# Two layers of a hybrid diffusion backbone on one core: the residual stream between the layers

## The chip, the core and the metric

The kernel runs on one core of one Trainium2 chip. Time is device time in microseconds (us). Three runs of the kernel before took 932.32, 935.01 and 936.65 us; their median, 935.01 us, is the number that the change is measured against. Everything is in float32.

## The reference

There are 256 context tokens and 256 latent tokens of width 1024, and two layers. Each layer is a mixer (layer 0: convolution and pooling; layer 1: two kinds of attention) and then a mixture of experts, both with a normalisation that is scaled and shifted by conditioning vectors ahead, and a gated residual behind. The part that matters here is the end of layer 0 and the start of layer 1, where the experts' output is added to the residual stream and the sum is normalised, scaled and shifted again:

```python
y2 = moe(jnp.concatenate([h2c, h2l], axis=1), router_w, router_b,
         moe_w_gate[i], moe_w_up[i], moe_w_down[i])
xc = xc + mod_c[5] * y2[:, :n_ctx]
xl = xl + mod_l[:, 5] * y2[:, n_ctx:]
# next layer
mod_l = (c_act @ mod_w[i] + mod_b[i]).reshape(b, N_MOD, 1, d)
hl = modulate(rms_norm(xl, norm_g[i, 0]), mod_l[:, 0], mod_l[:, 1])
```

The experts stand in 8 groups of 4. A token goes to one group, and in it to two experts. So each of the 512 rows of the residual is added to by exactly one group.

## The kernel before, in words

The weights are the bulk of the traffic. The queue of SP (SyncE) loads them in the order of a list, `STREAM`, 2 MB a unit, into seven slots of a ring and into buffers lent for a time: `X` (which holds the residual in the mixers and an expert's weights in the expert phase), `B`, and pieces of `hT`, `GB`, `MR` and `WORK`. Before each load SP waits for the last user of the slot. SP works strictly in order: whatever one load waits for holds up all that stand behind it.

In the expert phase of layer 0 the residual lies in DRAM. `save_rows` writes it to the tensor `x_old` before `X` is lent out. For each group the rows of its tokens, up to 64 in a first tile and 64 in a second, are gathered, multiplied by the group's gate and up matrices (`gate_up`, L1329) and by its down matrices (`down`, L1354) on PE. A tile lies as 128 partitions: partition 0 to 63 hold the first halves of 64 rows and 64 to 127 the second halves. `out_rows` on DVE then scales the product by the output gate (L2225) and adds the old rows (L2231), which GpSimd has gathered from `x_old` (`take_old`, L897). GpSimd scatters the new rows into a second DRAM tensor, `x_new` (`put_new`, L904). Both are indirect DMAs on GpSimd's queue. A group whose second tile is empty skips it by a branch on every engine (`late_second`). A scatter and a gather are issued for the second tile all the same; their rows are out of bounds and move nothing.

When all eight groups are stored and the branch for overfull groups is passed (`overflow_pool`, not taken with these inputs), GpSimd raises `moe_done`. SP waits for that with the loads of `X` from `x_new` (L1037), which stand in its order ahead of `("oin", "ckv")`, the first projection weights of layer 1. The two loads `("mod", 1, 1, 0)` and `("mod", 1, 1, 1)`, the scale vector's weights of layer 1, stand ahead of that wait and are issued while the experts still run.

Then layer 1 begins. ACT squares the four tiles of `X` (L1564) and copies the product of the scale weights (`mod_copy(7)`, L1570) between the second and the third tile; GpSimd forms the inverse root of the mean square (L2346, L2347); DVE scales the tiles (L1972) and forms the norm's scale (L1931, L1965). PE multiplies the scale weights (`mod(7)`, L1075, 16 trace rows for each 2 MB half), turns their product into columns (L1085), turns the scaled tiles into 16 blocks (L1125), and ACT and DVE copy the blocks out by turns with scale and shift (`hcols`, L1591 and L1995). The first projection of layer 1 (L497) needs all 16 blocks of the first stretch. PE's order there is `mod(7)` first, then the blocks.

## Time and profile before

| | |
|---|---|
| median of the three runs | 935.01 us |
| profiled execution | 934.93 us |
| its span (first to last instruction) | 933.2 us |
| PE busy | 833.0 us (89%) |
| DVE, ACT, POOL busy | 371.4, 164.6, 170.7 us |
| DMA over the span | 317 GB/s mean, 296.08 MB |
| granted TensorE clock, mean | 0.954 |

The profile comes from one execution. Times in its rows count from the start of the span; the execution is 1.7 us longer than the span. PEclk is the granted TensorE clock as a share of full speed: 1.00 is 2.4 GHz and 0.50 is 1.2 GHz. PE appears in two rows, the multiplications (PE) and the weight loads that overlap them (PEld); a name with a q behind it (SPq, POOLq) is the engine's sequencer or the DMAs that it issues. In the bracket at the end of a timeline row stand the idle time of that engine before the row and what ended it.

### The profile page before, as it was taken

What the parts mean: (1) busy time and instruction counts of PE and PEld (TensorE: products, weight loads), DVE (VectorE), ACT (ScalarE), POOL (GpSimd) and SP (SyncE); (2) the same over time, 40 slices, a digit from 0 to 9 for tenths busy, and PEclk for the clock granted to TensorE, in tenths of its full rate; (3) what the DMA queues carried; (4) which work ended last, traced back from release to release, by engine and by line L of the source; (5) the groups of instructions that cost most, each with busy time, mean ns of one, the idle gap of its engine ahead of it and who ended that gap; (6) DMA issues with size and microseconds to landing.
All of it is one profiled execution on the core that took longest, in us unless ns stands there. A gap on an engine that the chain in (4) does not pass through costs nothing.

```text
span 933.2 us, 9923 instructions
## 1 busy us (share of the span) xinstructions
PE 833.0 (89%) x3695; PEld 369.4 (40%) x3695; DVE 371.4 (40%) x785; ACT 164.6 (18%) x409; POOL 170.7 (18%) x205
## 2 busy tenths in 40 slices
PE   4899999999999999887949999979897999979785
PEld 2444445447433333222318544536545333322221
DVE  1279998216121212110114488457645122212110
ACT  2301012216100000000013111436612000000000
POOL 2100292131120222201122231320220100000000
PEclk9999999999999999898967999989996999999999
DMA  8999355627999999999979467521294899999994
GB/s 362 409 418 403 135 210 218 270 90 245 330 399 424 352 399 399 400 396 416 424 299 428 185 260 292 249 91 40 114 388 159 341 425 425 420 426 428 426 422 175
DMA packets 31463, 296.08 MB, mean 317 GB/s; under 512 B 6050, under 2 KB 6356, under 8 KB 13229
## 3 DMA queue, kind: packets, MB, share of 16 engines
q1 hardware_dynamic: 25200, 283.26, 75.0%
q0 software_dynamic: 6128, 12.02, 3.6%
q8 instruction: 38, 0.62, 0.3%
q14 instruction: 21, 0.16, 0.0%
q10 hardware_dynamic: 76, 0.02, 0.0%
HBM read 291.84 MB, written 11.53 MB: 325 GB/s over the span
## 4 chain that ended last, share of the span: by engine, by line
PE 52%; DMA 18%; DVE 13%; issue 6%; SPq 4%; ACT 2%; PEld 2%; POOL 1%; another core or an unknown queue 0%; PEldq 0%; DVEq 0%; POOLq 0%; ACTq 0%
PE bank L1329 15%; DVE WORK L2301 10%; PE bank L497 9%; PE bank L1354 6%; PE bank L1479 5%; DMA WORK<-in_gu_pack 5%; DMA ring<-in_gu_pack 4%; DMA ring<-in_down_pack 4%; DMA ring<-in_win_pack 3%; PE bank L1191 3%; SPq L1016 2%; PE bank L1426 2%; PE bank L1267 2%; DMA WORK<-x_old,smalli 1%; PE bank L554 1%
## 5 line engine op out<-in xcount | busy, mean ns | idle before, releaser
L1329 PE MATMUL bank<-ring,WORK 128*64 128x512 f32 x352 | 107.3, 627 | 12.0 <-DMA ring<-in_gu_pack 7.5
L1329 PE MATMUL bank<-ring,hT 128*64 128x512 f32 x352 | 108.0, 616 | 3.7 <-issue 2.2
L2301 DVE SCALAR_TENSOR_TENSOR WORK<-WORK,par 128x512 f32<-128x512 f32 x116 | 90.7, 861 | 0.0
L497 PE MATMUL bank<-ring,hT 128*128 128x512 f32 (+2 forms) x256 | 88.0, 499 | 0.7 <-ACT hT L1591 0.7
L1354 PE MATMUL bank<-ring,WORK 128*64 128x512 f32 x336 | 76.3, 596 | 2.3 <-DMA ring<-in_down_pack 1.2
L2210 DVE SCALAR_TENSOR_TENSOR hT<-hT,WORK,bank 128x256 f32<-128x256 f32 x18 | 8.7, 481 | 167.4 <-ACT hT L1628 161.1
L2210 DVE SCALAR_TENSOR_TENSOR WORK<-WORK,bank 128x256 f32<-128x256 f32 x16 | 7.7, 481 | 137.3 <-ACT WORK L1628 137.3
L1633 ACT ACTIVATE WORK<-bank 128x256 f32<-128x256 f32 x34 | 13.1, 384 | 268.3 <-PE bank L1338 268.3
L497 PEld LDWEIGHTS bank<-ring,hT 128*128 128x128 f32 x256 | 46.0, 190 | 35.9 <-issue 34.0
L1426 PE MATMUL bank<-hT,ring 128*128 128x512 f32 x128 | 57.7, 610 | 2.0 <-DMA ring<-in_win_pack 2.0
L1479 PE MATMUL bank<-ring,B 128*128 128x512 f32 x128 | 56.6, 596 | 0.8 <-DVE B L2318 0.8
L1329 PEld LDWEIGHTS bank<-ring,WORK 128*64 128x64 f32 x352 | 31.7, 143 | 61.6 <-issue 61.3
L1329 PEld LDWEIGHTS bank<-ring,hT 128*64 128x64 f32 x352 | 31.8, 141 | 45.0 <-issue 44.8
L2346 POOL TENSOR_SCALAR small<-small 128x1 f32<-128x1 f32 (+2 forms) x46 | 13.5, 294 | 182.7 <-DVE small L1792 62.6
L1075 PE MATMUL bank<-ring,cs 128*32 128x512 f32 x256 | 34.1, 670 | 9.5 <-DMA ring<-in_mod_pack 8.3
L1329 PE MATMUL bank<-WORK,hT 128*64 128x512 f32 x72 | 36.1, 649 | 7.3 <-issue 5.7
L904 POOL DMA_INDIRECT latents<-WORK,smalli x8 | 8.1, 1014 | 181.8 <-DVE WORK L2231 153.1
L1354 PEld LDWEIGHTS bank<-ring,WORK 128*64 128x64 f32 x336 | 23.2, 137 | 45.2 <-issue 40.6
L1426 PEld LDWEIGHTS bank<-hT,ring 128*128 128x128 f32 x128 | 24.6, 194 | 33.6 <-issue 31.3
L891 POOL DMA_INDIRECT hT<-h_rows,smalli x14 | 13.4, 960 | 129.7 <-PE bank L1303 56.0
L2347 POOL TENSOR_TENSOR small<-small,cst 128x1 f32<-128x1 f32 (+2 forms) x46 | 36.1, 785 | 3.8
L1479 PEld LDWEIGHTS bank<-ring,B 128*128 128x128 f32 x128 | 23.8, 190 | 31.2 <-issue 27.7
(337 smaller groups left out, 1215.5 us busy)
## 6 DMA issues: line engine op xcount, KB each, us to landing
ring<-in_gu_pack SPq DMA_DIRECT2D x39, 2048.0 KB, 20.5
ring<-in_mod_pack SPq DMA_DIRECT2D x24, 2048.0 KB, 12.2
ring<-in_down_pack SPq DMA_DIRECT2D x19, 2048.0 KB, 24.9
WORK<-in_gu_pack SPq DMA_DIRECT2D x5, 2048.0 KB, 22.9
ring<-in_wout_pack SPq DMA_DIRECT2D x4, 2048.0 KB, 12.1
ring<-in_gu_pack SPq DMA_DIRECT2D x8, 1024.0 KB, 34.8
ring<-in_win_pack SPq DMA_DIRECT2D x3, 2048.0 KB
X<-in_gu_pack SPq DMA_DIRECT2D x3, 2048.0 KB
```

What stands on the lines that cost most here:

```text
L497: mm = pe.matmul(dst[:, 0:hi - lo], hT[:, k, t * P:(t + 1) * P], w[:, k, :], start=k == 0, stop=k == KC - 1)
L1016: sp.dma_start(dst, src).then_inc(sem(f"weights_in{at}"), 16)
L1075: mm = pe.matmul(bank[b][at:at + 32, :], cs[:, k, :], w, start=k < 2, stop=k >= KC - 2)
L1191: mm = pe.matmul(bank[OUT_BANKS[L][i % 2]][:, :], lhs(k, j), w[:, k, :], start=k == 0, stop=k == KC - 1)
L1267: mm = pe.matmul(bank[7 - 7 * h][:, w * k:w * k + w], X[:, 2 + t, at:at + P] if L else B[:, t * D + at:t * D + at + P], FIRST[:, w * t:w * ...
L1329: mm = pe.matmul(dst[ST * x:ST * x + ST, :], HG[L][s][:, k, :], columns(units[x], 512 * k, 512), start=k == 0, stop=k == KC - 1)
L1354: mm = pe.matmul(bank[5 + s][ST * h:ST * h + ST, :], HET[s][:, f, ST * x:ST * x + ST], columns(n, 2048 * x + 1024 * f + 512 * h, 512), sta ...
L1426: mm = pe.matmul(b[:, :], w[:, k, 256 * part + P * (m % 2):256 * part + P * (m % 2) + P], hT[:, k, :], start=k == 0, stop=k == KC - 1)
L1479: mm = pe.matmul(bank[OUT_BANKS[0][i % 3]][:, :], mixT[:, (k + 4) % KC, j * P:(j + 1) * P], w[:, (k + 4) % KC, :], start=k == 0, stop=k == ...
L2210: dve.scalar_tensor_tensor(out=T1[L][s], in0=SG[L][s], scalar=cwt[:, at:at + 1], in1=src[:, 0:DE], op0=ALU.mult, op1=ALU.mult).then_inc(se ...
L2301: ins = dve.scalar_tensor_tensor(out=acc, in0=src, scalar=w, in1=acc, op0=ALU.mult, op1=ALU.add)
L2347: pool.tensor_tensor(dst, dst, C("half", 0, 1).to_broadcast([P, n]), ALU.pow).then_inc(sem(name), 1)
```

## The change

Three things are done. First, the rows of groups 0 to 6 are scattered back into the tensor that they were gathered from (now `x_rows`), and `x_new` is gone; GpSimd stores seven groups, not eight, and raises `moe_done` after the seventh. Second, SP's wait for `moe_done` and the reload of `X` stand ahead of `("mod", 1, 1, 0)`, with a wait for the last expert unit that lay in `X`. Third, the rows of group 7 never go to DRAM: DVE builds one-hot matrices from the token numbers of the group's tiles (`last_places`, eight comparisons of 128x128, after group 6's rows), PE multiplies them with the gated rows (`spread_last`: eight products of 64 rows by 128 tokens by 512 columns, 16 where the second tile is in use), and DVE adds the eight results, 128x512 each, to the reloaded `X`.

What follows from it in the orders: PE turns the first four blocks of the scaled tiles ahead of `mod(7)`; ACT squares all four tiles ahead of `mod_copy(7)`; DVE scales all four tiles ahead of the norm's scale. Group 7's gather of old rows, its addition (L2231) and its scatters are gone. The overflow branch gets a buffer of its own and a few waits; it is not taken.

The diff, cut to its core:

```diff
-        xa = nc.dram_tensor("x_old", (TOK, D), F32, kind="Internal").ap()
-        xb = nc.dram_tensor("x_new", (TOK, D), F32, kind="Internal").ap()
+        xa = nc.dram_tensor("x_rows", (TOK, D), F32, kind="Internal").ap()
...
+        LAST_HOT = [hw[:, 1024 + 512 * i:1536 + 512 * i] for i in (0, 1)]
+        last_tok = csg[:, 0:2]
+        SPREAD = [(t, h) for t in range(NT) for h in (0, 1)]
+        SPREAD_BANKS = (0, 1, 2, 3, 4, 5, 7, 6)
...
# SP
-                if u == ('oin', 'ckv'):
-
+                if u == ("mod", 1, 1, 0):
+                    done, v = freed(max(i for i in range(n) if PLACES[i][0] == X_SLOT))
+                    expert_slot_freed(sp, 0, done, v)
                     sp.wait_ge(sem("moe_done"), 1)
                     for t in range(NT):
-                        sp.dma_start(X[:, t, :], xb[t * P:(t + 1) * P, :]).then_inc(sem(("x_in", "x_back")[t // 2]), 16)
+                        sp.dma_start(X[:, t, :], xa[t * P:(t + 1) * P, :]).then_inc(sem(("x_in", "x_back")[t // 2]), 16)
                 load(n, load_sources(u) if u[0] not in ("gu", "down") else expert_sources(u[1], u[2], n, u[0]))
...
# PE
+            def spread_last():
+
+                def products(tiles):
+
+                    for n, (t, h) in enumerate(SPREAD):
+                        half = slice(ST * h, ST * h + ST)
+                        for i in range(tiles):
+                            mm = pe.matmul(bank[SPREAD_BANKS[n]][:, :], LAST_HOT[i][half, t * P:t * P + P], YO[i][half, :], start=i == 0, stop=i == tiles - 1)
+                        mm.then_inc(sem("ln_turned"), 1)
 
                 for i in range(2):
-                    turn_pair(tag, i, range(KC))
+                    pe.wait_ge(sem(f"y_used_{i}"), GROUPS)
+                last = second_tile(pe, 0, GROUPS - 1)
+                with pe.If(last > 0):
+                    products(2)
+                with pe.Else():
+                    products(1)
+                pe.nop()
...
             overflow_pe(pe, 0)
-
+            spread_last()
+
+            turn_pair("a1", 0, range(4))
             mod(7)
-            turn_x("a1")
+            turn_pair("a1", 0, range(4, KC))
+            turn_pair("a1", 1, range(KC))
...
# ACT
-            square_rows("a1", (0, 1))
+            square_rows("a1", range(4))
             mod_copy(7)
-            square_rows("a1", (2, 3))
...
# DVE
+                    if L == 0 and g == GROUPS - 1:
+                        return
                     if L == 0:
                         dve.wait_ge(sem(f"old_in_{s}"), 16 * g + 16)
...
+                def last_places():
+
+                    for i in range(2):
+                        for t in range(NT):
+                            ins = ts(LAST_HOT[i][:, t * P:t * P + P], C("iota128"), last_tok[:, i:i + 1], float(NOROW - t * P), ALU.subtract, ALU.is_equal)
+                    link(ins)
...
             overflow_vector(dve, 0)
+            for n, (t, h) in enumerate(SPREAD):
+                dve.wait_ge(sem("ln_turned"), 2 * NT + n + 1)
+                dve.wait_ge(sem(("x_in", "x_back")[t // 2]), (96, 32)[t // 2])
+                x = X[:, t, 512 * h:512 * h + 512]
+                tt(x, x, bank[SPREAD_BANKS[n]][:, :], ALU.add).then_inc(sem("x_added"), 1)
             norm_rows("a1")
...
# GpSimd
-                for g in range(GROUPS):
+                for g in range(GROUPS - 1 + L):
                     if L == 0 and g + 2 < GROUPS:
                         gather(g + 2)
                     store(g)
-                    if L == 0 and g + 1 < GROUPS:
+                    if L == 0 and g + 2 < GROUPS:
                         old_rows(g + 1)
```

SP's order at the end of layer 0 and the start of layer 1, before. The two units `in_mod_pack` are the scale weights of layer 1, `in_oin_pack` are its projections:

```order
L1012 DMA ring<-in_down_pack 128x2048 [waits gu_done_1,gu_done_0]
L1013 DMA ring<-in_down_pack 128x2048
L1016 DMA ring<-in_mod_pack 128x4096 [waits down_done_1,down_done_0]
L1016 DMA ring<-in_mod_pack 128x4096 [waits gu_done_1,gu_done_0]
L1037 DMA X<-x_new 128x1024 [waits moe_done]
L1037 DMA X<-x_new 128x1024 x3
L1016 DMA ring<-in_oin_pack 128x1536 [waits down_done_1,down_done_0]
```

And of the changed kernel:

```order
L1021 DMA ring<-in_down_pack 128x2048 [waits gu_done_1,gu_done_0]
L1022 DMA ring<-in_down_pack 128x2048
L1047 DMA X<-x_rows 128x1024 [waits moe_done,gu_done_1,gu_done_0]
L1047 DMA X<-x_rows 128x1024 x3
L1025 DMA ring<-in_mod_pack 128x4096 [waits down_done_1,down_done_0]
L1025 DMA ring<-in_mod_pack 128x4096 [waits gu_done_1,gu_done_0]
L1025 DMA ring<-in_oin_pack 128x1536 [waits down_done_1,down_done_0]
```

The reload and its wait have gone past the two scale weight units, which now stand behind both.

PE's order between the experts' last branch and the first blocks, before (`weights_in4` and `weights_in3` are the two halves of the scale weights, `xs` counts scaled tiles):

```order
L842 UNCONDITIONAL_BRANCH
L1075 MATMUL bank<-ring,cs 32x512 [waits weights_in4,mod_rows]
L1075 MATMUL bank<-ring,cs 32x512 x7
L1075 MATMUL bank<-ring,cs 32x512 [waits weights_in3]
L1075 MATMUL bank<-ring,cs 32x512 x7
L1085 MATMUL bank<-cst,MR 128x4 [waits mod_cols,mod_rows]
L1085 MATMUL bank<-cst,MR 128x4 x3
L1125 MATMUL bank<-cst,B 128x128 [waits xs]
L1125 MATMUL bank<-cst,B 128x128 x7
L1125 MATMUL bank<-cst,B 128x128 [waits ht_0]
```

And of the changed kernel:

```order
L765 TENSOR_LOAD smalli [waits y_used_1,y_used_0]
L765 ISA x2
L1151 COMPARE_AND_BRANCH
L1145 MATMUL bank<-WORK,hT 128x512 x16
L1151 UNCONDITIONAL_BRANCH
L1145 MATMUL bank<-WORK,hT 128x512 x8
L1153 UNCONDITIONAL_BRANCH
L1135 MATMUL bank<-cst,B 128x128 [waits xs]
L1135 MATMUL bank<-cst,B 128x128 x7
L1085 MATMUL bank<-ring,cs 32x512 [waits weights_in4,mod_rows]
L1085 MATMUL bank<-ring,cs 32x512 x7
L1085 MATMUL bank<-ring,cs 32x512 [waits weights_in3]
```

Ahead of the scale weights' product now stand a branch, the eight or sixteen spreading products and the first eight transposes, with their waits for group 7's rows and for two scaled tiles.

## Rows read from the trace of the kernel before

**Rows 1.** Chain that ended last, 452 to 500: start, us, what.
```profile
456.46 1.00 POOL x_new L904
457.77 11.33 DMA WORK<-x_old,smalli
...
472.41 5.28 DMA x_new<-WORK,smalli
...
478.67 6.59 DMA X<-x_new
...
485.29 2.19 ACT B L1564 x4
...
498.29 0.57 ACT hT L1591
...
499.37 0.73 PE bank L497 x3
```

**Rows 2.** Timeline of PE, 440 to 512: start, us, engine, line, op, count.
```profile
464.54 3.65 PE L1354 MATMUL bank<-ring,WORK 128*64 128x512 f32 x16 [0.56 <-ACT WORK L1633]
471.15 2.89 PE L1075 MATMUL bank<-ring,cs 128*32 128x512 f32 x16 [2.96 <-DMA ring<-in_mod_pack]
477.08 3.64 PE L1075 MATMUL bank<-ring,cs 128*32 128x512 f32 x16 [3.05 <-DMA ring<-in_mod_pack]
...
493.73 4.96 PE L1125 MATMUL bank<-cst,B 128*128 128x128 f32 x22 [1.61 <-DVE hT L1995]
```

**Rows 3.** Timelines of ACT and of DVE in the same stretch.
```profile
487.38 0.57 ACT L1570 ACTIVATE MR<-bank 128x512 f32<-128x512 f32 x1
...
490.51 0.56 ACT L1591 ACTIVATE hT<-bank,mods,gsc 128x256 f32<-128x256 f32 x1 [0.47 <-PE bank L1125]
...
494.88 0.56 ACT L1591 ACTIVATE hT<-bank,mods,gsc 128x256 f32<-128x256 f32 x1 [2.16 <-PE bank L1125]
...
462.25 0.75 DVE L2222 SCALAR_TENSOR_TENSOR WORK<-GB,WORK 128x512 f32<-128x512 f32 x1 [0.68 <-DMA x_new<-WORK,smalli]
468.31 0.69 DVE L2225 TENSOR_TENSOR WORK<-bank,WORK 128x512 f32<-128x512 f32 x1 [5.31 <-PE bank L1354]
...
491.81 1.41 DVE L1972 TENSOR_SCALAR B<-X,small 128x1024 f32<-128x1024 f32 x1 [0.72 <-POOL small L2347]
```

**Rows 4.** The scatter that GpSimd issues at 456.46: KB, us to landing.
```profile
x_new<-WORK,smalli POOLq DMA_INDIRECT x1, 9.1
```

**Rows 5.** SP's timeline of DMA issues, 340 to 520.
```profile
439.84 2.47 SPq L1016 DMA_DIRECT2D ring<-in_mod_pack  x2
...
480.41 3.56 SPq L1016 DMA_DIRECT2D ring<-in_oin_pack  x5
```

**Rows 6.** The reload of X: issue ns, first and last start, landing.
```profile
L1037 SPq DMA_DIRECT2D X<-x_new x4: 327/432/693, 478.3 to 479.9; - x4
...
DMA to landing us min/median/max: 3.2/6.5/7.9
```

**Rows 7.** Stretches: length, busy by engine, then PEclk, DMA share, GB/s.
```profile
464.00:470.00 6.00, 3.65 (x16) 1.23 (x16) 1.11 (x2) 0.38 (x1) 0.00 (x0) 1.00 1.03 426
472.00:475.00 3.00, 2.03 (x12) 0.27 (x4) 0.00 (x0) 0.00 (x0) 1.11 (x2) 0.50 0.75 301
475.00:479.00 4.00, 1.92 (x12) 0.59 (x16) 0.00 (x0) 0.00 (x0) 0.00 (x0) 0.50 0.08 28
479.00:484.00 5.00, 1.73 (x12) 0.00 (x0) 0.00 (x0) 0.00 (x0) 0.00 (x0) 0.50 0.92 251
484.00:490.00 6.00, 1.99 (x10) 1.99 (x11) 1.59 (x3) 4.71 (x9) 2.78 (x6) 0.50 1.03 425
```

**Rows 8.** Timeline of PE around 160: the same multiplication earlier, both halves.
```profile
160.28 3.64 PE L1075 MATMUL bank<-ring,cs 128*32 128x512 f32 x32
```

**Rows 9.** PE's groups of instructions at 617 to 660: busy, mean ns.
```profile
L563 PE MATMUL bank<-B,WORK 64*128 64x512 f32 x32 | 9.0, 641 | 0.0
```

**Rows 10.** Timeline of PE at 423 to 424: a wait behind a branch.
```profile
423.94 1.09 PE L1329 MATMUL bank<-WORK,hT 128*64 128x512 f32 x1 [5.71 <-issue]
```

More of the change, by code:

```diff
@@ L375, in generator_kernel @@
         rcol = wk[:, 2092:2114]
-        ROWS_IN = (("old_in_0", 16 * GROUPS), ("old_in_1", 16 * GROUPS), ("gathered_0", 16 * (GROUPS - 1)))
+        ROWS_IN = tuple((name, 16 * (GROUPS - 1)) for name in ("old_in_0", "old_in_1", "gathered_0"))
         FIRST = YO[0]
@@ L841, in overflow_pe @@
                         mm.then_inc(sem(f"over_down{L}"), 1)
+                    if L == 0:
+                        pe.wait_ge(sem("over_rows0"), j + 2)
             with pe.Else():
@@ L876, in overflow_vector @@
                     if L == 0:
-                        gate = YO[0]
+                        gate = OYO
                         dve.scalar_tensor_tensor(out=gate, in0=GM[1], scalar=msk[:, bass.ds(j + 8 * c, 1)], in1=GM[0],
@@ L880, in overflow_vector @@
                         dve.wait_ge(sem(f"over_t1{L}"), steps * j + 3)
-                    dve.tensor_tensor(YO[0], bank[5][:, :], gate, ALU.mult).then_inc(sem(f"over_t1{L}"), 1)
+                    y = (OYO, YO[0])[L]
+                    dve.tensor_tensor(y, bank[5][:, :], gate, ALU.mult).then_inc(sem(f"over_t1{L}"), 1)
                     dve.wait_ge(sem(f"over_t1{L}"), steps * j + steps)
-                    dve.tensor_tensor(YO[0], YO[0], XR[L][0], ALU.add).then_inc(sem(f"over_rows{L}"), 1)
+                    dve.tensor_tensor(y, y, XR[L][0], ALU.add).then_inc(sem(f"over_rows{L}"), 1)
             with dve.Else():
@@ L898, in take_old, with put_new @@
                                            bounds_check=2 * rows_ - 1, oob_is_err=False)
-        def put_new(pool, L, s, i):
+        def put_new(pool, L, src, i):
             rows_ = moe_plan(L)[0] * P
-            dst = (xb, out[0])[L].rearrange(HALVES, h=2)
-            return pool.indirect_dma_start(dst, bass.IndirectOffsetOnAxis(ap=smalli[:, i:i + 1], axis=0), YO[s], None,
+            dst = (xa, out[0])[L].rearrange(HALVES, h=2)
+            return pool.indirect_dma_start(dst, bass.IndirectOffsetOnAxis(ap=smalli[:, i:i + 1], axis=0), src, None,
                                            bounds_check=2 * rows_ - 1, oob_is_err=False)
@@ L909, in overflow_pool @@
             with pool.If(n > 0):
+                if L == 0:
+                    pool.wait_ge(sem("hg_turned_0"), turned_by(0, GROUPS - 1))
                 with pool.Fori(0, n) as j:
@@ L1018, in save_rows @@
             def save_rows(L):
-                sp.wait_ge(sem("x_added"), (8, 12)[L])
+                sp.wait_ge(sem("x_added"), (8, 20)[L])
                 for j, t in enumerate(x_tiles(f"m{L}")):
@@ L1977, in norm_rows @@
                 if tag == "a1":
-                    for j in (0, 1):
+                    for j in range(4):
                         scaled(tag, j)
@@ L1981, in norm_rows @@
                     norm_scale(1, 0)
-                    for j in (2, 3):
-                        scaled(tag, j)
                 for i in range(2):
@@ L2033, in add_out @@
                         if i >= 2:
-                            dve.wait_ge(sem("x_added"), 8 * L + i - 1 + last)
+                            dve.wait_ge(sem("x_added"), 16 * L + i - 1 + last)
                         if L == 1 and i < 2:
@@ L2166, in route @@
                 if L == 0:
+                    dve.tensor_copy(last_tok, bank[6][:, GROUPS * c - c:GROUPS * c])
                     ts(smalli[:, 4:4 + ntile], bank[6][:, 0:ntile], float(NOROW), None, ALU.add)
@@ L2218, in out_rows @@
                     if G0 + g:
-                        dve.wait_ge(sem(f"y_stored_{s}"), 16 * (G0 + g))
+                        dve.wait_ge(sem(f"y_stored_{s}"), 16 * ((GROUPS - 1) * L + g))
                     if L == 0:
@@ L2251, in experts @@
                             late_second(g - 1)
+                        if L == 0 and g == GROUPS - 1:
+                            last_places()
                     if L == 1 and q == 0 and g + 1 < GROUPS:
@@ L2384, in store @@
                     for s in range(c):
-                        pool.wait_ge(sem(f"y_rows_{s}"), 8 * L + g + 1)
-                        put_new(pool, L, s, 48 + g * c + s).then_inc(sem(f"y_stored_{s}"), 16)
+                        pool.wait_ge(sem(f"y_rows_{s}"), (GROUPS - 1) * L + g + 1)
+                        put_new(pool, L, YO[s], 48 + g * c + s).then_inc(sem(f"y_stored_{s}"), 16)
                 def old_rows(g):
@@ L2390, in old_rows @@
                         if g:
-                            pool.wait_ge(sem(f"y_rows_{s}"), 8 * L + g)
-                            pool.wait_ge(sem(f"old_in_{s}"), 128 * L + 16 * g)
+                            pool.wait_ge(sem(f"y_rows_{s}"), g)
+                            pool.wait_ge(sem(f"old_in_{s}"), 16 * g)
                         take_old(pool, L, s, 48 + g * c + s).then_inc(sem(f"old_in_{s}"), 16)
@@ L2405, in take_group @@
                     if g > 2:
[L2406 removed]
+                        pool.wait_ge(sem("y_rows_0"), GROUPS - 1 + g - 2)
                     take_old(pool, 1, g % 3, 48 + g).then_inc(sem(ROWS_IN[g % 3][0]), 16)
@@ L2426, in experts @@
                 for s in range(c):
-                    pool.wait_ge(sem(f"y_stored_{s}"), 128 * (L + 1))
+                    pool.wait_ge(sem(f"y_stored_{s}"), 16 * (GROUPS - 1 + GROUPS * L))
                 overflow_pool(pool, L, n)
```

13 lines of the change are left out of this document (6 added, 7 removed).

## The prediction, made before the changed kernel was run

> **What bounds the kernel now.** I read first the chain that ended last, because the change touches one seam of the program and only the chain says what the seam costs. Between the last experts and layer 1 it runs through single transfers, not through a busy engine [rows 1]: a scatter of group 6 at 456.46, a gather of old rows behind it that takes 11.33 us, the scatter of group 7 at 472.41 that takes 5.28, the reload of X (6.59), two squares on ACT, and then the blocks up to the first projection at 499.37. The DVE timeline shows that the gather is no price of its own: group 7's product is ready for DVE only at 468.31, when PE has ended its last down product [rows 2, 3], and the gather came 1.1 us later. What the seam really costs is everything between 468.2 and 499.37, some 31 us in which PE does little.
>
> The second view is the PE timeline, since the change also moves the scale weights of layer 1. PE waited for each of their 2 MB halves, until 471.15 and until 477.08, though SP had issued both by 442.3 [rows 2, 5]. The third view, the stretches, says why [rows 7]: the DMA engines move 426 GB/s in 464 to 470 and run dry only around 475. So the queue is full of expert weights until shortly before, and the scale weights are what fills it from then to 475. Then it stands empty until the reload starts (28 GB/s in 475 to 479). The scale product ended at 480.7 but its copy stood on ACT behind two squares until 487.38 [rows 3]. In the old kernel the scale weights thus have 6.7 us of slack, and the rows are late.
>
> **The change part by part.** Every time below is in the profiled execution, 934.93 us (span 933.2 and 1.7 around it); the median of the runs shown is 935.01, so the two can be exchanged within 0.1.
>
> *Part 1, moe_done earlier.* The stores of group 6 now end the expert phase. The second starts at 456.46 and lands 9.1 us later, at 465.6 [rows 4]; the first has landed by 462.25, where DVE's wait for it ended [rows 3]. Group 7's scatter, in an almost idle queue, took 5.28 [rows 1]. So the second store lands between 462.3 (just behind the first) and 465.6. The queue stays loaded until about 463.8 (475 minus the 4.19 MB of scale weights and 0.4 MB of the rest at the rates of rows 7), so I take 464.8, near the loaded row. From landing to SP's first issue it was 0.6 us (472.41 + 5.28 = 477.7 to 478.3 [rows 1, 6]). The reload starts at 465.4, bounds 462.9 and 466.2, instead of 478.3: 12.9 us earlier.
>
> *Part 2, the scale weights behind the reload.* They are issued 26 us later than before, and the queue order puts X's 2.10 MB ahead of them. From its first issue at 478.3 the old reload had moved at most 5 x 251 GB/s = 1.26 MB by 484, and the other 0.84 MB at 425 GB/s takes 2.0 us: 7.7 us in all [rows 7]. The 4.19 MB of scale weights follow at 425: 9.9 us. From the last byte to PE's start was 2.1 us before (about 475 to 477.08). So the second half is there at 465.4 + 7.7 + 9.9 + 2.1 = 485.1, the first 4.9 earlier, at 480.2. Before, it was 477.08: the scale weights lose 8.0 us, more than their slack. Bounds: DMA without a gap from 463.8 and all 6.29 MB at 425 gives 463.8 + 14.8 + 2.1 = 480.7; reload at 466.2 and X at 251 GB/s throughout (0.7 to start, 8.4 to move) gives 487.3.
>
> Beside that row stands a rule of the Trainium skill, "DMA: Bandwidth & Descriptors", section on the anatomy of one DMA: a transfer costs about 2.0 us plus its bytes at 436 GB/s, whatever it is. By it the reload and the weights together would take an estimated 16.4 us and arrive at 481.8, so that the time would be 3.3 us lower than my sum. The row of 251 GB/s while X's rows are read speaks against it, the 2.1 us at the end speaks for it.
>
> *Part 3, from the scale weights to the projection.* The product of the second half took 3.64 us at the half clock (0.50 in 475 to 479, 1.2 GHz); earlier in the kernel both halves together took 3.64 [rows 2, 8], so 1.82 at full clock. PE will again have waited just before it, as in the nearer row: I take 3.64. Copy to the first block on ACT: 487.38 to 490.51, 3.13, and 0.1 for PE to ACT. The blocks go at 494.88 to 498.29 in four steps, 0.85 each; eight blocks per engine take 7 x 0.85 + 0.56, and 0.5 more until PE starts, 7.0 in all. Before it was 8.9 (490.51 to 499.37), because DVE scaled the last tile at 491.81 and PE waited 1.61 for its block [rows 2, 3]; all four tiles are now scaled early, which gives 1.9 back. The projection starts at 485.1 + 3.64 + 0.1 + 3.13 + 7.0 = 499.0, against 499.37.
>
> *Part 4, group 7's rows on chip.* YO is gated at 469.0 (468.31 + 0.69). The branches on DVE and on PE I cost like GpSimd's from landing to SP, 0.6 each: first product at 470.2. Eight products are 16 trace rows of 64 x 512; 32 such rows were 9.0 us busy [rows 9], so 4.5 us, or 9.0 at the half clock. The granted clock fell while PE idled at the same place, so I take the middle, to about 477. The last tile of X lands by 9.5 us after the first issue (7.9 behind the last issue [rows 6]), at 474.9, so it waits for nothing. The last addition, 0.7 like any 128x512, ends at 477.7; two scaled tiles at 0.75 make 479.2; eight transposes at 4.96 / 22 make 481.0. The first half of the scale product, which stands behind them on PE, is done at 484.6 at worst. That is 0.5 us ahead of the second half's arrival: hidden, but barely. If all products run at the half clock it is 1.7 us too late, at full clock 2.8 early.
>
> *Free edits.* The eight comparisons on DVE lie between group 6's rows and 460.6, where DVE otherwise idles behind PE; without that cover they would be about 2 us. Group 7's gather and scatters are off the queue, each at most 64 rows of 4 KB, 0.6 us at 425 GB/s. The loads of the projections, before issued at 480.41 [rows 5], come right behind the scale weights, about 2 us earlier than before, and PE did not wait for them. Everything behind the first projection moves with it, since the loads there are triggered by PE's own progress.
>
> Sum: 499.0 - 499.37 = -0.4 us, 934.5. Bounds of this case: 480.7 and full clock, 492.6 (-6.7); 487.3 and half clock, 501.2 (+1.8).
>
> **The rivals.** *Early data.* The store lands right behind the first one, X flows at the full 425 GB/s since its queue never runs dry, and PE keeps its clock through the products. Then the second half is there at 480.7 and the projection starts at 492.7: -6.7, 928.3. For it speaks that the queue was idle only because nothing was issued; against it the measured 251 GB/s under the reload, and the clock that fell to 0.50 at this place with the same idle time ahead [rows 7].
>
> *A stall at the new branch (slower).* At 423.94 PE stood 5.71 us behind a branch with nothing that the profile names as its reason [rows 10]; the queue was full then, as it will be at 470 with X in flight. If PE's sequencer stands like that at the branch in the spreading, the transposes and the first half of the scale product move 5.7 us back, to 490.3, and the second half follows at 3.64: projection at 504.2, +4.8. With all products at the half clock 2.3 more: +7.1, 942.0. It decides from 0.5 us of delay on, and most other branches on PE passed without such a stall.
>
> *The change moves work, not the end.* That is my forecast itself: the scale weights take the place of the rows.
>
> **How the numbers follow.** My forecast has a chance of 0.68, the early data 0.18, the stall 0.14. What a measurement can tell from no change is about 0.5%, 4.7 us; the forecast lies inside it but for its lowest bound, which is the first rival; the two rivals lie outside. So faster 0.18, same 0.68, slower 0.14. The range reaches half way into either rival: 929.0 to 940.0. The likeliest case's own range is 931.5 (second half 3 us sooner, or the scale product at full clock and 1 us sooner) to 937.
>
> **What would show it.** SP's reload would start near 465.4 and the two scale units right behind it. PE's second half of L1075 (its line in the new kernel is L1085) would start near 485, ended by a DMA, and the copy on ACT would follow it at once, not behind squares. The products would stand at 470 to 477, the four additions of late tiles would wait for PE and not for X, and the wait of PE for DVE between the blocks would be gone. Wrong would be: a reload that starts before 463, a second half before 482, or an idle stretch of PE over 3 us between the last down product and the first spreading product. And should a wait in layer 1 absorb or add to a shift at the first projection, the end of the run would not follow it; the rows show none.

## The result, and the profile after

The changed kernel took 927.99 us (median of 6 runs, 926.33 to 931.1), the kernel before 934.20 beside it (6 runs). The ratio is 0.9936, with a 95% interval of 0.9921 to 0.9950: 6.0 us faster, and no less than 4.7. A second measurement of it on another chip (after_again, below) gave 0.9949, 0.9931 to 0.9967: some 4.8 us. The prediction, 934.5 and most likely no change, was wrong; its range ended at 929.0. One run of e3_one_product, below, took 2340.01 us and is left out of that kernel's ratio, not of its median. The profiled execution of the changed kernel took 929.5 us (span 927.7, mean granted clock 0.962), 5.4 less than the profiled one of before.

The chain of waits of the changed kernel, 454 to 500, shows what stands in place of the chain of before [rows 1]. Columns: start, us, what.

```profile
456.92 6.85 DMA x_rows<-WORK,smalli
...
464.42 0.33 SPq L1047
...
466.95 17.19 DMA ring<-in_mod_pack
...
484.18 1.97 PE bank L1085 x16
...
486.17 0.60 ACT MR L1597
...
486.82 1.07 PE bank L1095 x8
...
488.40 0.57 ACT hT L1618
...
494.47 5.60 PE bank L501 x33
```

The gather, the second scatter, the reload and the squares have left the chain. Group 6's store, SP's reload, the second half of the scale weights, its product, and the blocks stand there instead, as Parts 1 to 3 of the prediction have it. But the first projection starts at 494.47, not at 499.0; before it was 499.37 [rows 1]. Behind it nothing is given back: the span is shorter by 5.5 us, the start of the first projection by 4.9.

The store at the head of this chain carries nothing: it is that of group 6's second tile, which is empty (both stores of the group moved 0.22 MB, and a full tile is 0.26). DVE's wait for the first store ended at 462.52, 1.2 us before the second landed:

```profile
462.52 0.75 DVE L2247 SCALAR_TENSOR_TENSOR WORK<-GB,WORK 128x512 f32<-128x512 f32 x1 [0.54 <-DMA x_rows<-WORK,smalli]
```

What waiting for the empty store costs isn't shown; no run leaves it out.

PE in the same stretch, with the idle time ahead of a row and what ended it in the bracket. L1378 is the last down product, L1145 the spreading products, L1135 the blocks (L1125 before), L1085 the two halves of the scale product (L1075 before), L1095 its turning (L1085 before), L501 the first projection (L497 before):

```profile
464.95 3.68 PE L1378 MATMUL bank<-ring,WORK 128*64 128x512 f32 x16 [0.56 <-ACT WORK L1660]
470.86 5.40 PE L1145 MATMUL bank<-WORK,hT 64*128 64x512 f32 x16 [2.24 <-issue]
479.04 1.97 PE L1135 MATMUL bank<-cst,B 128*128 128x128 f32 x8 [2.78 <-DVE B L1998]
480.94 2.60 PE L1085 MATMUL bank<-ring,cs 128*32 128x512 f32 x16
484.18 1.92 PE L1085 MATMUL bank<-ring,cs 128*32 128x512 f32 x16 [0.64 <-DMA ring<-in_mod_pack]
486.82 1.05 PE L1095 MATMUL bank<-cst,MR 128*128 128x4 f32 x8 [0.72 <-ACT MR L1597]
489.11 4.68 PE L1135 MATMUL bank<-cst,B 128*128 128x128 f32 x24 [1.24 <-ACT hT L1618]
494.47 7.71 PE L501 MATMUL bank<-ring,hT 128*128 128x192 f32 x46 [0.69 <-ACT hT L1618]
```

The second half of the scale product takes 1.92 us where it took 3.64 [rows 2]. The stretches of the changed kernel (columns as in [rows 7]; the two numbers behind the engines' are the granted clock and the DMA share) show at which clock:

```profile
472.00:475.00 3.00, 3.00 (x10) 1.11 (x10) 2.57 (x4) 1.36 (x3) 0.33 (x2) 0.52 1.04 437
...
477.00:479.00 2.00, 0.00 (x0) 0.00 (x0) 1.98 (x4) 1.79 (x4) 1.19 (x2) 0.99 0.96 410
479.00:481.00 2.00, 1.96 (x12) 1.63 (x16) 0.86 (x2) 0.00 (x0) 1.69 (x3) 0.50 1.09 467
...
483.00:485.00 2.00, 1.36 (x16) 0.29 (x12) 0.00 (x0) 0.00 (x0) 0.00 (x0) 1.00 1.02 428
485.00:487.00 2.00, 1.28 (x14) 0.31 (x6) 0.00 (x0) 0.60 (x1) 0.00 (x0) 1.00 1.03 436
...
489.00:492.00 3.00, 2.89 (x14) 2.92 (x15) 1.52 (x4) 2.02 (x4) 0.66 (x1) 0.53 1.03 437
```

Before, the clock stood at 0.50 in every stretch from 472 to 490, and the DMA engines stood nearly still in 475 to 479 [rows 7]. Now the DMA engines move over 400 GB/s there, and the clock is 1.00 from 483 to 487: just when the second half and its turning run. Ahead of that PE had blocks and the first half to do without a gap from 479.04 to 483.5; which of its work brings the clock back is asked of the experiments.

SP's issues and the four late additions on DVE answer to [rows 5, 6] and to Part 4:

```profile
464.42 1.90 SPq L1047 DMA_DIRECT2D X<-x_rows  x4
466.41 0.91 SPq L1025 DMA_DIRECT2D ring<-in_mod_pack  x2
467.42 3.06 SPq L1025 DMA_DIRECT2D ring<-in_oin_pack  x5
```

```profile
472.02 1.28 DVE L2368 TENSOR_TENSOR X<-X,bank 128x512 f32<-128x512 f32 x2 [2.58 <-PE bank L1145]
...
475.18 2.48 DVE L2368 TENSOR_TENSOR X<-X,bank 128x512 f32<-128x512 f32 x4 [0.42 <-PE bank L1145]
```

SP issues the reload at 464.42 and the two scale units right behind it. The additions wait for PE, not for X, and end at 477.66, where 477.7 was forecast.

### The profile page after: what moved, and what is told of

Its sections match the earlier page's. It is cut to its first block, busy times and chain, and to the rows that moved or that the text cites. A ratio compares the mean times of both kernels' runs of the same rounds, so it can differ in the third digit from the quotient of the medians.

```text
span 927.7 us, 9974 instructions
## 1 busy us (share of the span) xinstructions
PE 835.6 (90%) x3711; PEld 369.9 (40%) x3711; DVE 376.5 (41%) x801; ACT 164.6 (18%) x409; POOL 166.6 (18%) x201
## 4 chain that ended last, share of the span: by engine, by line
PE 54%; DMA 20%; DVE 13%; issue 5%; SPq 3%; ACT 2%; PEld 2%; POOL 0%; another core or an unknown queue 0%; PEldq 0%; DVEq 0%; POOLq 0%; ACTq 0%
PE bank L1353 15%; DVE WORK L2337 10%; DMA ring<-in_gu_pack 9%; PE bank L501 9%; PE bank L1378 6%; PE bank L1503 5%; DMA WORK<-in_gu_pack 5%; DMA ring<-in_win_pack 3%; PE bank L1215 3%; SPq L1025 2%; DMA ring<-in_mod_pack 2%; PE bank L1450 2%; PE bank L1291 2%; PE bank L558 1%; PE bank L567 1%
## 5 line engine op out<-in xcount | busy, mean ns | idle before, releaser
L501 PE MATMUL bank<-ring,hT 128*128 128x512 f32 (+2 forms) x256 | 88.0, 500 | 0.7 <-ACT hT L1618 0.7
L1378 PE MATMUL bank<-ring,WORK 128*64 128x512 f32 x336 | 76.3, 596 | 1.0 <-ACT WORK L1660 1.0
L501 PEld LDWEIGHTS bank<-ring,hT 128*128 128x128 f32 x256 | 46.0, 190 | 35.7 <-issue 33.9
L1378 PEld LDWEIGHTS bank<-ring,WORK 128*64 128x64 f32 x336 | 23.1, 137 | 43.9 <-issue 40.6
L1450 PEld LDWEIGHTS bank<-hT,ring 128*128 128x128 f32 x128 | 24.6, 195 | 33.6 <-issue 31.2
L1085 PE MATMUL bank<-ring,cs 128*32 128x512 f32 x256 | 32.1, 637 | 4.0 <-DMA ring<-in_mod_pack 2.8
```

The lines of the kernel that those rows point to most:

```text
L501: mm = pe.matmul(dst[:, 0:hi - lo], hT[:, k, t * P:(t + 1) * P], w[:, k, :], start=k == 0, stop=k == KC - 1)
L1085: mm = pe.matmul(bank[b][at:at + 32, :], cs[:, k, :], w, start=k < 2, stop=k >= KC - 2)
L1378: mm = pe.matmul(bank[5 + s][ST * h:ST * h + ST, :], HET[s][:, f, ST * x:ST * x + ST], columns(n, 2048 * x + 1024 * f + 512 * h, 512), sta ...
L1450: mm = pe.matmul(b[:, :], w[:, k, 256 * part + P * (m % 2):256 * part + P * (m % 2) + P], hT[:, k, :], start=k == 0, stop=k == KC - 1)
```

## The experiments

I asked two things: is the gain due to the order on the queue (theory A), and where do the 4.5 us between 499.0 and 494.47 come from? For the clock I had three answers: the blocks and the first half, an unbroken run on PE, bring it back (B); the spreading products do (C, the rival); and whichever it is, without both the second half runs at the half clock as forecast (D; against it E, that the second half runs at the full clock whatever PE did before). Each kernel is timed against the kernel before on the same chip. In the table "gap" is the time from the end of the last down product to the first projection, in the one profiled execution of each.

| kernel | median, us | ratio to before, 95% | gap, us |
|---|---|---|---|
| before | 934.2 to 934.9 | 1 | 31.2 |
| e1_weights_first | 935.84 | 1.0013, 0.9998 to 1.0027 | 31.9 |
| e5_before_busy | 933.69 | 1.0001, 0.9980 to 1.0022 | 29.5 |
| e6_done_late | 933.88 | 0.9997, 0.9982 to 1.0013 | 29.0 |
| e4_products_twice | 932.72 | 0.9981, 0.9968 to 0.9994 | 26.5 |
| e7_half_ahead | 930.77 | 0.9949, 0.9932 to 0.9967 | 26.5 |
| e10_one_product_blocks_behind | 930.59 | 0.9951, 0.9933 to 0.9969 | 26.2 |
| changed kernel, first time | 927.99 | 0.9936, 0.9921 to 0.9950 | 25.8 |
| e11_banks_turned | 929.62 | 0.9953, 0.9935 to 0.9970 | 25.4 |
| e3_one_product | 929.27 | 0.9950, 0.9933 to 0.9967 | 24.7 |
| e2_blocks_behind | 928.74 | 0.9941, 0.9920 to 0.9961 | 24.1 |
| after_again (the changed kernel) | 929.81 | 0.9949, 0.9931 to 0.9967 | 23.3 |
| e8_half_ahead_blocks_behind | 927.29 | 0.9913, 0.9895 to 0.9931 | 22.8 |
| e8_again | 926.66 | 0.9917, 0.9899 to 0.9935 | 22.8 |

The gap orders the kernels nearly as their times do, so this stretch, the seam between the layers, is where they differ. It does so within some 3 us: the changed kernel itself has 25.8 and 23.3 in two executions.

**The order on the queue (e1_weights_first).** Everything changed, but the reload stands behind the scale weights again:

```diff
-                if u == ("mod", 1, 1, 0):
+                if u == ("oin", "ckv"):
```

> The changed kernel with SP's order of before: both halves of the scale weights are issued while the experts run, the reload of X behind moe_done. All else as changed. Theory A (the arrival of the scale weights, 19.7 us behind the first issue of the reload, ends the seam): the weights now arrive at about 471 and 477, X about 10 us later than in the changed kernel, last tile near 482; additions end near 483, two scaled tiles near 484.5, and PE's order (four blocks, then the scale product, 3.8 us at full clock) puts the first projection at 498 to 499, 3.5 to 4.5 us later than in the changed kernel, about 932. Rival (where the reload stands in SP's order is nothing, the rows stay on chip and that is the gain): first projection within 1 us of 494.5, about 928.

The whole gain is gone, more than theory A had forecast (about 932). In its timelines of DVE and of PE, group 7's additions now wait for X, and PE for the tiles:

```profile
479.14 5.02 DVE L2368 TENSOR_TENSOR X<-X,bank 128x512 f32<-128x512 f32 x8 [9.64 <-DMA X<-x_rows]
```

```profile
485.54 1.97 PE L1135 MATMUL bank<-cst,B 128*128 128x128 f32 x8 [10.92 <-DVE B L1998]
487.44 4.63 PE L1085 MATMUL bank<-ring,cs 128*32 128x512 f32 x32
```

The reload was issued at 466.72, as early as in the changed kernel within 2.3 us; it came late because 4.2 MB of scale weights lay ahead of it. Storing in place and spreading on chip are worth nothing without the order. The reverse, the order without the rows of group 7 on chip, wasn't run.

**The time of the release (e6_done_late).** `moe_done` is raised only once group 7's product is ready, 4.9 us later:

```diff
+                if L == 0:
+                    pool.wait_ge(sem("y_used_0"), GROUPS)
                 pool.sem_inc(sem("moe_done"), 1)
```

> The changed kernel, but GpSimd raises moe_done only when DVE has gated group 7's rows, so that the reload starts near 470 and not at 464.4: 5.5 us later, with nothing else changed. Theory A: everything behind follows one for one: second half of the scale weights 19.7 us behind the first issue, first projection 5 to 6 us later, near 500, time 933 to 934, the whole gain gone. Rival (PE's rows path through the products is the bound and the reload has slack): 0 to 2 us later.

The reload's first issue is at 469.31 (464.42 in the changed kernel), and PE's second half still waits for its weights:

```profile
487.20 1.92 PE L1085 MATMUL bank<-ring,cs 128*32 128x512 f32 x16 [0.90 <-DMA ring<-in_mod_pack]
...
497.31 4.95 PE L501 MATMUL bank<-ring,hT 128*128 128x192 f32 x29 [0.70 <-ACT hT L1618]
```

So the date of group 6's store goes through to the end, though not one for one: of the 4.9 us at the reload 3.0 are left at the second half, which came 17.9 us behind the first issue and not 19.8, and 2.8 at the projection. In the times the whole gain of some 6 us is gone. Profile and times differ mostly by which executions were profiled: the two, 932.76 and 929.5, are 3.3 us apart, but e6's lies 1.1 us under its kernel's median and the changed kernel's 1.5 over its own.

**How much the rows can be late (e4_products_twice).** PE does the spreading products twice:

```diff
-                    for n, (t, h) in enumerate(SPREAD):
+                    for again in (0, 1):
+                        for n, (t, h) in enumerate(SPREAD):
...
```

> The changed kernel with all eight spreading products computed twice into the same banks; the additions wait for the second. It measures what slack the rows have behind the scale weights (the forecast: 0.5 us). Theory A with that slack: the products end 4 us later, near 480, the additions near 481.5, the blocks and the first half move by 3.5 to 4 us, the second half starts at 487 to 488 behind PE's own work, first projection 2.5 to 3.5 us later, time about 931. Rival (the scale weights alone end the seam, the rows have several us of slack): within 1 us of the changed kernel.

```profile
471.90 7.14 PE L1146 MATMUL bank<-WORK,hT 64*128 64x512 f32 x32 [2.22 <-issue]
...
483.77 5.34 PE L1085 MATMUL bank<-ring,cs 128*32 128x512 f32 x32
```

The two halves of the scale product now run without a wait for DMA: the rows are late, as was expected. The projection starts 3.6 us later than in after_again on the same chip, the median is 2.9 higher, for products that end 3.8 later. So the slack there is some 0.2 us, and the forecast of 0.5 was the right size.

**What brings the clock back (e2, e3, e10).** e2 puts the blocks behind the scale product, so that PE has no transposes ahead of it. e3 makes one spreading product only, whose bank all eight additions read, so that seven products are left out of the result; e10 does both.

```diff
# e2, e10
-            turn_pair("a1", 0, range(4))
+            pe.wait_ge(sem("x_added"), 16)
             mod(7)
-            turn_pair("a1", 0, range(4, KC))
+            turn_pair("a1", 0, range(KC))
# e3, e10
-                    for n, (t, h) in enumerate(SPREAD):
+                    for n, (t, h) in enumerate(SPREAD[:1]):
...
```

> The changed kernel with PE's order of before at one place: the whole scale product ahead of the blocks (PE waits for all eight additions first, because the product's banks are those of the last two), and no block turned early. Theory B (the run of transposes and the first half of the product just ahead of the second half brings the granted clock back to 1.00, and that is worth 2.6 us of product and turning): without the transposes the first half runs alone and PE waits longer before the second; granted clock 0.50 in the second half, which takes 3.6 us and the turning 1.9, first projection 2.5 to 4 us later than 494.5. Rival (the clock follows the spreading products, which are still there): second half at 1.9 us, only the four blocks in front are lost, 0.5 to 1 us later.

> The changed kernel with one of the eight spreading products; all eight additions read its bank, so the other seven products are left out of the result. PE is then idle from about 471.5 until the first blocks near 478. Theory B: the clock of the second half comes from the run of blocks and first half, not from the products, so it is full there as before (1.9 to 2.4 us) and the first projection stays within 1 us of 494.5. Rival C (the products keep the clock up for the scale product): granted clock 0.50 through the second half, 3.6 us, turning 1.9, first projection 2.5 to 3.5 us later although the additions end earlier.

> Both of the last two edits at once in the changed kernel: one spreading product whose bank all eight additions read (seven products left out of the result), and the whole scale product ahead of the blocks. PE then idles from about 471.5 to 478 and again between the two halves, as the forecast had assumed. Theory D (either run of PE work, the products or the blocks with the first half, keeps the granted clock at 1.00 for the second half, and the forecast's mis-sized term is that half at 3.64 us with the turning at 1.87): now the clock is 0.50, second half 3.6, turning 1.9, first projection 2.5 to 3.5 us later than with the products (492.7), at 495 to 496.5. Rival E (the second half runs at full clock here whatever PE did before): 1.9 us, first projection within 0.7 us of 492.7.

PE of e2, of e3 and of e10, from the scale product to its turning, and behind the dots a stretch in which the second half runs:

```profile
478.30 1.92 PE L1085 MATMUL bank<-ring,cs 128*32 128x512 f32 x16 [2.05 <-DVE X L2368]
482.69 1.92 PE L1085 MATMUL bank<-ring,cs 128*32 128x512 f32 x16 [2.47 <-DMA ring<-in_mod_pack]
485.33 1.06 PE L1095 MATMUL bank<-cst,MR 128*128 128x4 f32 x8 [0.72 <-ACT MR L1597]
...
483.00:485.00 2.00, 1.61 (x16) 0.26 (x8) 0.00 (x0) 0.32 (x1) 0.00 (x0) 1.00 1.03 435
```

```profile
481.76 4.89 PE L1085 MATMUL bank<-ring,cs 128*32 128x512 f32 x32
487.38 1.05 PE L1095 MATMUL bank<-cst,MR 128*128 128x4 f32 x8 [0.73 <-ACT MR L1597]
...
485.00:487.00 2.00, 1.65 (x16) 0.24 (x8) 0.00 (x0) 0.27 (x1) 0.00 (x0) 1.00 1.09 459
```

```profile
479.22 3.64 PE L1085 MATMUL bank<-ring,cs 128*32 128x512 f32 x16 [6.22 <-DMA ring<-in_mod_pack]
484.06 3.40 PE L1085 MATMUL bank<-ring,cs 128*32 128x512 f32 x16 [1.20 <-DMA ring<-in_mod_pack]
488.19 1.06 PE L1095 MATMUL bank<-cst,MR 128*128 128x4 f32 x8 [0.72 <-ACT MR L1597]
...
485.00:487.00 2.00, 2.00 (x16) 0.31 (x8) 0.00 (x0) 0.00 (x0) 0.00 (x0) 0.50 1.14 482
```

e2 shows that B is not needed: with the products alone the clock is 1.00 in its stretches from 475 to 487, and both halves take 1.92. The delay of the projection that both answers expected isn't seen (492.74, against 494.47 and 492.57 of the changed kernel). e3 shows that C is not needed either: its clock is 0.50 from 475 to 483, while PE waits for the rows until 479.86 and then starts on the blocks, and back at 1.00 from 485, after the blocks and the first half; the two halves take 4.89 together, where 7.04 is e10's sum. Take both away and D comes true for the second half: the clock of e10 is 0.50 from 475 to 487, and the second half takes 3.40 us, near the 3.64 of the forecast. So either of two things that the change itself gives PE to do brings the clock back ahead of the second half. D's other half fails: the turning was to take 1.9 us and took 1.06, at a clock of 0.98 in 487 to 489. So the lost clock costs e10 time in the second half alone. e10 is 1.85 us slower than e2, both timed on one chip; the second half's own difference is 3.40 - 1.92 = 1.5. The two intervals overlap, so the size rests on the durations.

**The clock alone (e5_before_busy).** The kernel before, with 20 small products on PE between the scale product and its turning, to bring the clock back without the change:

```diff
-            mod(7)
+            mod_multiply(7)
+            for i in (0, 1):
+                pe.wait_ge(sem(f"y_used_{i}"), GROUPS)
+            busy(5, 20)
+            mod_turn(7)
```

> The kernel before, with 20 small products (128x128 with a constant) on PE between the scale product and its turning, where PE idled for 6.7 us behind the squares; nothing else changed. It measures the granted clock by itself. Theory D: the clock is 1.00 when the turning starts, so it takes 1.05 and not 1.87, and blocks are turned at full clock: first projection 0.8 to 1.5 us earlier than 499.37, time 0 to 1.5 us below the kernel before. So the clock alone is no more than a third of the gain in the old order, since there the rows are late. Rival (the clock is most of the gain): 3 us or more.

Its PE (lines as in the kernel before):

```profile
484.23 1.05 PE L1085 MATMUL bank<-cst,MR 128*128 128x4 f32 x8 [0.22 <-ACT MR L1574]
...
490.83 4.96 PE L1125 MATMUL bank<-cst,B 128*128 128x128 f32 x22 [2.09 <-DVE hT L1999]
```

The turning runs at the full clock, but the blocks still wait for DVE's copies, which stand behind its late tiles, and the clock is 0.50 again from 487 on. The ratio is 1.0001, give or take 0.2%. The gap is 1.7 us shorter in this execution, but its chain doesn't pass through the turning: it goes through the third tile of X, and from that tile's square to the projection it takes 11.1 us, against 11.5 in the kernel before. What the clock shortened here wasn't on the path; it counts only once the scale product bounds the end.

**A finer order (e7, e8, e8_again, after_again, e11).** The first half of the weights needn't be loaded behind the reload. e7 lets it go ahead of the reload; e8 does that and takes the PE order of e2:

```diff
-                if u == ("mod", 1, 1, 0):
+                if u == ("mod", 1, 1, 1):
```

> The changed kernel with the first half of the scale weights issued ahead of the wait for moe_done and only the second half behind the reload. Theory A: the DMA queue no longer stands idle between 463.5 and 466, the second half arrives 2 to 3 us sooner; but PE does four blocks and the first half before it (479 to 483.5), so the first projection gains only 0.6 to 1 us: 493.5 to 494, 927 to 928. Rival (the reload now waits behind the first half and the rows become the bound): X 4 to 5 us later, first projection 1 to 3 us later.

> The last kernel with, in addition, the whole scale product ahead of the blocks on PE. Theory A: the first half is there before the additions end near 478, the second at 479 to 481, so that the product ends near 482, the scale is ready at 485 and the first projection starts at 490.5 to 492, 2.5 to 4 us before the changed kernel's 494.5; time 924.5 to 926.5, below both kernels. Rival (rows are the bound once X waits behind the first half): first projection 493 to 495, no better than the changed kernel.

In e7 the rival comes true, the rows become the bound: the additions wait 4.62 us for X, until 474.90, and PE's first blocks wait for DVE until 481.26. The second half is there early, but stands on PE behind blocks that aren't ready. e8 takes that away, since the scale product runs while DVE and ACT work on the rows. I ran it again beside the changed kernel on another chip:

> The changed kernel itself, on the chip of the next three. Theories A and D: seam and time as in its first profile: second half of the scale weights 18 to 20 us behind the first issue of the reload, both halves at mostly full clock, first projection 494 to 495.5, about 928, ratio 0.993 to 0.995. Rival (the first profile was a lucky execution): 930 or more.

```profile
471.50 3.70 PE L1145 MATMUL bank<-WORK,hT 64*128 64x512 f32 x16 [2.22 <-issue]
...
483.51 1.96 PE L1085 MATMUL bank<-ring,cs 128*32 128x512 f32 x16 [0.16 <-DMA ring<-in_mod_pack]
```

The second half again runs at the full clock; the spreading products, 5.40 us in the first profile, take 3.70. The median, 929.81, lies between theory and rival, and the profiled execution is the fastest of the six.

> The kernel with the first half of the scale weights ahead of the reload and the whole scale product ahead of the blocks, next to the changed kernel. Theory A: 1 to 3 us below the changed kernel. Rival: within 0.5 us of it.

```profile
479.72 5.23 PE L1085 MATMUL bank<-ring,cs 128*32 128x512 f32 x32 [2.94 <-DVE X L2368]
485.68 1.05 PE L1095 MATMUL bank<-cst,MR 128*128 128x4 f32 x8 [0.73 <-ACT MR L1597]
...
491.99 8.04 PE L501 MATMUL bank<-ring,hT 128*128 128x192 f32 x48 [0.69 <-ACT hT L1618]
```

e8 took 926.66 us against 929.81 for the changed kernel on that chip, 3.1 less, and was the fastest on both chips. The intervals of the two ratios overlap a little (0.9899 to 0.9935, and 0.9931 to 0.9967). The products for the scale no longer wait for a transfer but for the additions (2.94 us), because the scale product writes a bank that the additions read until then, and PE waits for all eight of them.

e11 turns the banks so that the wait goes, and lets the scale product start after two of the eight additions (`x_added` already stands at 8 when they begin):

```diff
-        SPREAD_BANKS = (0, 1, 2, 3, 4, 5, 7, 6)
+        SPREAD_BANKS = (6, 7, 0, 1, 2, 3, 4, 5)
...
+            pe.wait_ge(sem("x_added"), 10)
```

> The kernel before in this list with one thing more: the spreading products use banks 6, 7, 0 to 5 in this order, so that the banks of the scale product are those of the first tile's additions, and PE waits for two additions ahead of the scale product and not for eight. Theory A: the first half starts near 477 and not at 480.3, the second ends at 482.5 to 483.5, the scale is ready near 485, and the first projection starts 1.5 to 2.5 us earlier, at 490 to 491; time 1 to 2.5 us below that kernel. Rival (the additions and the squares of the last tile are the bound once X waits behind the first half): no earlier projection, PE waits for the blocks of the second stretch instead.

```profile
475.79 1.92 PE L1085 MATMUL bank<-ring,cs 128*32 128x512 f32 x16
481.15 2.96 PE L1085 MATMUL bank<-ring,cs 128*32 128x512 f32 x16 [3.43 <-DMA ring<-in_mod_pack]
484.80 1.87 PE L1095 MATMUL bank<-cst,MR 128*128 128x4 f32 x8 [0.70 <-ACT MR L1597]
486.53 6.44 PE L1135 MATMUL bank<-cst,B 128*128 128x128 f32 x32
```

```profile
483.00:485.00 2.00, 1.30 (x9) 0.20 (x2) 0.00 (x0) 0.60 (x1) 0.00 (x0) 0.50 1.02 434
```

The first half starts 3.9 us earlier than in e8_again, the turning 0.9, and the projection 1.7 later (493.65). The last down product had ended 0.9 earlier in this execution, so counted from there the turning is no earlier at all and the projection 2.6 later. Neither theory A nor its rival came: the median is 929.62, 3.0 above e8_again on the same chip. With the first half done early PE idles 3.43 us ahead of the second; the clock is 0.50 from 483 to 492, and turning and blocks take 1.87 and 6.44 us where e8_again has 1.05 and some 4.7. What looked like a wait to be removed was what kept the two halves together on PE.

## Why the prediction was wrong, by its own steps

*Part 1, the release: the mechanism right, one term too large.* The store was to land 8.3 us after its issue (464.8 - 456.46), near the loaded row; it took 6.85. The queue ran dry sooner than I had worked out: the DMA engines moved 275 GB/s in 462 to 464 already. Part of that was a slip in the sum: at the rates of the old trace, with 377 GB/s in 470 to 472, the 4.6 MB reach back to 463.1 and not to 463.8. The reload started at 464.42 instead of 465.4, inside the bounds: 1.0 us.

*Part 2, the order on the queue: right.* From the reload's first issue to the second half it was to be 19.7 us; it was 19.76 (484.18 - 464.42). In the other executions with this order and a wait for the weights it was between 17.9 (e6) and 20.1 (e10), so that it agrees to 0.1 us is luck. The rule of the Trainium skill that stood beside this sum ("DMA: Bandwidth & Descriptors", on the anatomy of one DMA, which gives it for DMAs that GpSimd issues, while SP issued these) gives an estimated 16.4 us; no run came so low. e1 shows the price of the other order.

*Part 3, from the weights to the projection: this is the step that failed, in three of its terms.* It took the second half at 3.64 because "PE will again have waited just before it, as in the nearer row". PE did wait just before it, but only 0.64 us, and what counts is what it did before that: blocks and first half without a gap, and before these the spreading products, all of it work that the change had put there. The second half ran at a clock of 1.00 in 1.92 us: 1.7 us less. e10, without that work, has 3.40.

The second term is the way from the copy to the first block, 2.23 us (486.17 to 488.40) and not 3.13, 0.9 less. The 3.13 was read where the turning of the old kernel ran at the half clock, after PE had idled behind ACT's squares (e5, with products in that gap, has 1.05):

```profile
488.01 1.87 PE L1085 MATMUL bank<-cst,MR 128*128 128x4 f32 x8 [7.28 <-ACT MR L1570]
```

The forecast itself had the copy follow the product at once, and left the price as it was; PE idled 0.72 us there, and the turning took 1.05. This term doesn't hang on the clock of the second half: in e10, too, the way takes 2.23 (487.54 to 489.77).

The third: the blocks to the projection took 6.07 and not 7.0, though their clock was 0.53. Four of the sixteen were turned already, so the first two copies on each engine went out within 1.0 us; I had charged each engine eight steps of 0.85. Together with Part 1 this is 1.0 + 1.7 + 0.9 + 0.9 = 4.5, which is 499.0 - 494.5.

The first two of these four stood in the forecast as the lower end of its likeliest case, 931.5 ("the scale product at full clock and 1 us sooner"). Both came true. The other two, priced nowhere, bring this execution down to 929.5, the edge of the range, and the median of its kernel lies 1.5 lower: 6.5 us below the forecast. The second median, 929.81, lies just inside the range. after_again shows an execution in which the blocks too ran at the full clock, with the projection at 492.57.

*Part 4, the rows on chip: right.* Products to 476.26, last addition to 477.66, the first four blocks' turn to 481.0 and the first half to 483.5, against 477, 477.7, 481.0 and 484.6. The slack was 0.64 us, 0.5 by forecast, and e4 shows that it is no more than that order of size. The middle that was taken for the products held by luck, too: they took 5.40 us here, and 3.70 at the full clock in after_again, where 4.5 had been charged for it.

*The rivals.* The early data had a chance of 0.18 and a time of 928.3, which is where the kernel came out, but mostly for other reasons. The full clock in the second half was right (1.92 us). The data ready 4.4 us sooner was not: it was 0.9. The clock kept through the products was not, in this execution: it was 0.52 in 472 to 475, and came back later. I had tied early data and clock together, and outside that rival the clock had only the end of a range.

The stall at the new branch didn't come: the 2.2 us between the last down product and the first spreading product were 2.0 by forecast (468.2 to 470.2), 2.2 to 2.3 in all executions of the changed kernel and its variants. None of the signs that were to show the forecast wrong came, and those that were to show it right did, within 1 us: none of them was the clock of the second half or the price of the turning.

*Left open.* Why the last down product ends between 468.2 and 470.1 in executions of kernels that are the same up to there, and why the spreading products, behind the same wait of 2.2 us, keep the full clock in some executions (3.70 us in after_again, e1 and e7) and lose it for a time in others (5.40 in the first profile, e6, e8 and e11).

## What to carry to other kernels

A duration taken from the old kernel carries that stretch's granted clock with it: before it is put into a sum, ask what the engine will have done just ahead of it in the new order, and give the clock a case of its own. When two streams share one queue, add up the bytes that stand ahead of each and find the order in which both arrive with little to spare; here the same edits were worth nothing or 5 to 6 us by the place of one wait. An idle wait of 3 us that is moved ahead of the last serial steps can cost more than it gave. And a forecast's signs of being wrong should include one for each term of its sum.

## What the runs showed of the hardware beyond that

The landing of group 6's second store follows what else the queues hold, though not by that alone, and though no row of it is in bounds. It took 9.1 us in the kernel before [rows 4] and 9.18 in e1, where SP's queue held the scale weights and stayed at over 400 GB/s; it took 6.85 in the changed kernel, whose queue ran dry behind 462. In e1 no gather stands behind the store, so the gather of before isn't needed for the long landing. But e8 had as full a queue in both its executions (426 and 439 GB/s in 462 to 464), and the store took 7.66 us in one and 9.13 in the other; what made that difference stays open.

The granted clock of a stretch told little of what PE did in that same stretch. It was 0.50 in e10 in 485 to 487, where PE was busy throughout, and 1.00 in e1 in 475 to 479, where PE did nothing, behind a run of products. Nor is it enough that PE was busy before: in e11 the clock was 0.50 from 485 to 492, with PE at the turning and the blocks all that time.
